# Layer 1's attention: the next unit's maxima taken before this unit's normalising, and a differential unit's first factor moved to its output rows

## The reference

```
def attend(q, k, v, scale):        # per block of 128 queries
    s = einsum('bqhd,bkhd->bhqk', qi, k) * scale
    p = softmax(s)
    return einsum('bhqk,bkhd->bqhd', p, v)

o_m = attend(q_m, k_m, v_m, MLA_SCALE)
a1  = attend(q1, k1, v_d, DIFF_SCALE)
a2  = attend(q2, k2, v_d, DIFF_SCALE)
o_d = rms_norm(a1 - lam * a2, g_sub) * (1 - lam_init)
y   = concat([o_m, o_d]) @ w_out
```

## Time and profile before

| | |
|---|---|
| median of 3 runs | 958.49 us (957.53 to 961.4) |
| profiled execution, span from first to last instruction | 954.8 us |
| PE busy | 851.6 us (89%) |
| DVE busy | 323.4 us (34%) |
| ACT busy | 170.0 us (18%) |
| the attention, from its first score matmul to the first of the output projection | 617.8 to 688.2 us |

### The profile page before, as it was taken

One profiled execution on the slowest core, in us unless ns is written; L12 is line 12 of the kernel. 1 busy time (PEld: TensorE's weight loads), 2 busy tenths in 40 slices (PEclk: granted clock), 3 DMA queues, 4 the chain that ended last, 5 costly groups with the idle time before them and its releaser, 6 DMA issues.

```text
span 954.8 us, 10284 instructions
## 1 busy us (share of the span) xinstructions
PE 851.6 (89%) x3887; PEld 376.0 (39%) x3887; DVE 323.4 (34%) x711; ACT 170.0 (18%) x419; POOL 170.5 (18%) x210
## 2 busy tenths in 40 slices
PE   4899999999999999868769999888899999779786
PEld 2444445447333333223257443354546333223222
DVE  1279997217111211111132441636405111011011
ACT  2301022115000000000042112445414000000000
POOL 2100391221220222220212211300110111011001
PEclk9899999999999999889969999999999999889898
DMA  9999454709999999999989024372657999999994
GB/s 362 408 414 388 152 211 186 300 35 324 328 407 405 372 400 375 420 400 417 374 361 387 1 100 165 135 307 107 281 230 265 381 406 409 418 418 425 413 418 180
DMA packets 33975, 298.00 MB, mean 312 GB/s; under 512 B 6560, under 2 KB 6866, under 8 KB 16252
## 3 DMA queue, kind: packets, MB, share of 16 engines
q1 hardware_dynamic: 26928, 283.26, 73.5%
q0 software_dynamic: 6912, 13.92, 4.1%
q10 hardware_dynamic: 76, 0.02, 0.0%
HBM read 293.66 MB, written 12.58 MB: 321 GB/s over the span
## 4 chain that ended last, share of the span: by engine, by line
PE 50%; DMA 21%; DVE 15%; issue 6%; ACT 3%; SPq 3%; PEld 2%; POOL 0%; another core or an unknown queue 0%; PEldq 0%; POOLq 0%; DVEq 0%
PE bank L1255 14%; DVE WORK L2156 9%; PE bank L473 9%; PE bank L1280 7%; DMA ring<-in_gu_pack 5%; PE bank L1405 5%; DMA B<-in_gu_pack 5%; DMA WORK<-in_gu_pack 4%; DMA ring<-in_win_pack 3%; PE bank L1133 3%; SPq L970 2%; PE bank L1352 2%; DVE small L1791 1%; PE bank L1029 1%; DMA h_rows<-B 1%
## 5 line engine op out<-in xcount | busy, mean ns | idle before, releaser
L1255 PE MATMUL bank<-ring,hT 128*64 128x512 f32 x688 | 210.5, 633 | 23.4 <-DMA ring<-in_gu_pack 16.6
L2070 DVE SCALAR_TENSOR_TENSOR hT<-hT,WORK,bank 128x256 f32<-128x256 f32 x34 | 16.3, 480 | 327.3 <-ACT hT L1556 327.3
L1255 PEld LDWEIGHTS bank<-ring,hT 128*64 128x64 f32 x688 | 62.1, 145 | 117.9 <-issue 117.7
L2156 DVE SCALAR_TENSOR_TENSOR WORK<-WORK,par 128x512 f32<-128x512 f32 x116 | 90.7, 861 | 0.0
L473 PE MATMUL bank<-ring,hT 128*128 128x512 f32 (+2 forms) x256 | 88.0, 499 | 0.7 <-ACT hT L1519 0.7
L1280 PE MATMUL bank<-ring,WORK 128*64 128x512 f32 x368 | 83.5, 595 | 1.6 <-ACT WORK L1561 1.6
L1255 PE MATMUL bank<-WORK,hT 128*64 128x512 f32 x128 | 59.8, 609 | 9.1 <-issue 7.6
L1561 ACT ACTIVATE WORK<-bank 128x256 f32<-128x256 f32 x34 | 13.1, 384 | 281.9 <-PE bank L1264 281.9
L1352 PE MATMUL bank<-hT,ring 128*128 128x512 f32 x128 | 58.4, 616 | 2.2 <-DMA ring<-in_win_pack 2.2
L473 PEld LDWEIGHTS bank<-ring,hT 128*128 128x128 f32 x256 | 46.0, 190 | 35.8 <-issue 34.0
L1029 PE MATMUL bank<-ring,cs 128*32 128x512 f32 x384 | 49.2, 638 | 9.5 <-DMA ring<-in_mod_pack 7.4
(11 more groups left out here) (297 smaller groups left out, 1039.1 us busy)
## 6 DMA issues: line engine op xcount, KB each, us to landing
ring<-in_gu_pack SPq DMA_DIRECT2D x38, 2048.0 KB, 22.3
ring<-in_mod_pack SPq DMA_DIRECT2D x24, 2048.0 KB, 12.8
ring<-in_down_pack SPq DMA_DIRECT2D x20, 2048.0 KB, 26.7
WORK<-in_gu_pack SPq DMA_DIRECT2D x6, 2048.0 KB, 32.7
ring<-in_wout_pack SPq DMA_DIRECT2D x4, 2048.0 KB, 15.7
ring<-in_gu_pack SPq DMA_DIRECT2D x8, 1024.0 KB, 28.0
ring<-in_win_pack SPq DMA_DIRECT2D x3, 2048.0 KB, 36.8
X<-in_gu_pack SPq DMA_DIRECT2D x3, 2048.0 KB, 30.3
```

The lines of the kernel that those rows point to most:

```text
L1255: mm = pe.matmul(dst[ST * x:ST * x + ST, :], HG[L][s][:, k, :], columns(units[x], 512 * k, 512), start=k == 0, stop=k == KC - 1)
L2070: dve.scalar_tensor_tensor(out=T1[L][s], in0=SG[L][s], scalar=cwt[:, at:at + 1], in1=src[:, 0:DE], op0=ALU.mult, op1=ALU.mult).then_inc(se ...
L2156: ins = dve.scalar_tensor_tensor(out=acc, in0=src, scalar=w, in1=acc, op0=ALU.mult, op1=ALU.add)
```

## The change

`maxima(0)` is taken before the loop, and iteration i on DVE becomes maxima(i+1), output_rows(i-2), normalize(i). `normalize` of a differential unit no longer scales the first map: it computes the second map's factor relative to the first (lam times the second reciprocal times the first sum) in one small instruction, and adds the second map to the unscaled first. The first map's factor `ri` goes to the output rows, which are multiplied by two factors in one instruction, and to the squares, as their input scale. The output rows of a differential unit therefore also wait for `probs_ready`.

```diff
@@ o_squares (ACT)
-                act.activation(OR[j], bank[5][:, 0:P], ACT.Square, accum_out=oss[:, j:j + 1]).then_inc(sem("o_squares"), 1)
+                u = 2 * (i % 4)
+                act.activation(OR[j], bank[5][:, 0:P], ACT.Square, scale=ri[:, u:u + 1], accum_out=oss[:, j:j + 1]).then_inc(sem("o_squares"), 1)
@@ normalize (DVE)
                 ins = dve.reciprocal(ri[:, u:u + 1 + d], es[:, o:o + 1 + d])
                 if d:
                     link(ins)
-                    tt(ri[:, u + 1:u + 2], ri[:, u + 1:u + 2], lam[:, 5:6], ALU.mult)
-                    link(ts(EX[:, i % 2, 0, :], EX[:, i % 2, 0, :], ri[:, u:u + 1], None, ALU.mult))
+                    link(dve.scalar_tensor_tensor(out=ri[:, u + 1:u + 2], in0=ri[:, u + 1:u + 2], scalar=lam[:, 5:6],
+                                                  in1=es[:, o:o + 1], op0=ALU.mult, op1=ALU.mult))
                     ins = dve.scalar_tensor_tensor(out=EX[:, i % 2, 0, :], in0=EX[:, i % 2, 1, :], scalar=ri[:, u + 1:u + 2],
                                                    in1=EX[:, i % 2, 0, :], op0=ALU.mult, op1=ALU.add)
@@ output_rows (DVE)
                 dve.wait_ge(sem("pv_mm"), i + 1)
+                dve.wait_ge(sem("probs_ready"), i + 1)
+                scale = ri[:, 2 * (i % 4):2 * (i % 4) + 1]
+                if i >= 2:
+                    dve.wait_ge(sem("o_turned"), i - 1)
                 if UNITS[i][0]:
                     dve.wait_ge(sem("o_rstd"), i - 7)
-                    scale = ors[:, i % 2:i % 2 + 1]
+                    ins = ts(OR[i % 2], bank[5][:, 0:P], scale, ors[:, i % 2:i % 2 + 1], ALU.mult, ALU.mult)
                 else:
-                    dve.wait_ge(sem("probs_ready"), i + 1)
-                    scale = ri[:, 2 * (i % 4):2 * (i % 4) + 1]
-                if i >= 2:
-                    dve.wait_ge(sem("o_turned"), i - 1)
-                ts(OR[i % 2], bank[5][:, 0:P], scale, None, ALU.mult).then_inc(sem("o_rows"), 1)
+                    ins = ts(OR[i % 2], bank[5][:, 0:P], scale, None, ALU.mult)
+                ins.then_inc(sem("o_rows"), 1)
+
+            maxima(0)
             for i in range(n_units + 2):
-                if i < n_units:
-                    maxima(i)
+                if i + 1 < n_units:
+                    maxima(i + 1)
                 if i >= 2:
                     output_rows(i - 2)
                 if i < n_units:
```

## The result

The changed kernel takes 983.8 us (median of 4 runs, 981.3 to 985.7) against 958.5 us (4 runs, 957.5 to 961.4). The ratio on record is 1.0255, with an interval of 1.0231 to 1.0280: some 25 us slower (24.4 by the ratio, 25.3 by the medians). The forecast was 974 us, with a range from 968.5 to 979.5. The sign and the new wait were right; the loss is 1.6 times the 15.8 us forecast.

What follows compares the result with a forecast made beforehand. The DVE-ACT chain (4.46 us a unit) was taken as the bound. Terms 15.7 - 2.4 - 0.6 + 2.6 + 0.4 + 0.1 = 15.8 us, added to 958.5, gave 974 us, range 968.5 to 979.5.

Steps and rivals of the forecast that it cites:

- The sign: Whole kernel: slower, given 91%, against 5% for same and 4% for faster.
- the new wait: Differential iterations 8 to 15: PE stands 1.96 us before values for output rows queued behind fresh maxima; +15.7 us.
- The latent units: Maxima of units 4 and 6 wait for fresh scores, output rows behind them: 1.31 us, twice; +2.6 us.
- Two factors in one scaling, the scaled squares: DVE output rows: 0.065 us in each of six places, +0.4 us; squares once at the end, +0.1 us.
- The scaling that went, at nothing: DVE's normalize in differential units: some 0.4 us saved each, counted as nothing because PE's stand covers it; 3.2 us at most.
- The sum of the waits: Attention up to the output projection's first matmul: 15.8 us later, 688.2 to 704.0 us.
- All of it reaches the end: Behind the attention: loads start later by the whole amount and cannot make it up, so all 15.8 us reach the span.
- The clock: PE in differential units: forecast keeps 2.4 GHz; rival has half the units at 1.2 GHz, 15 us more, 989 us, 6%.

Runs made afterwards that it cites:

- order_only: The kernel before with only DVE's order of the change, first map still scaled in normalize: 982.1 us, ratio 1.0258.
- rows_first: The changed kernel with output_rows(i-2) put before maxima(i+1) on DVE: 960.6 us, ratio 1.0013 to the kernel before.
- latent_order: The kernel before with DVE's order of the change in the latent units alone: 962.6 us, ratio 1.0033.
- factor_only: The changed kernel with DVE's old loop order, so only the factor is moved: 958.3 us against 958.2, ratio 1.0002.
- fillers: Matmuls nobody reads, added to the changed kernel on PE between scores and values in iterations 8 to 15: ratios 1.0204, 1.0189 and 1.0211 for seven, three and one.
- fill3: The changed kernel with three matmuls that nobody reads on PE in each of iterations 8 to 15: 975.5 us, ratio 1.0189 to the kernel before.
- fill7: The changed kernel with seven matmuls that nobody reads on PE in each of iterations 8 to 15: 977.3 us, ratio 1.0204 to the kernel before.
- fill1: The changed kernel with one matmul that nobody reads on PE in each of iterations 8 to 15: 978.3 us, ratio 1.0211 to the kernel before.

## Why the prediction missed

**The new wait: right.** The step from "DVE's maxima of unit i+1 need fresh scores" to "PE stands about 2 us before its values" came out as worked. The brackets of the rows say 1.98 us in the first three iterations and 2.11 in the others, 16.4 us in eight waits. Counted as in the prediction, from the scores' start less 1.06 us, it is 2.05 (651.29 - 648.18 - 1.06) and 2.17 (670.61 - 667.38 - 1.06), where 1.96 and some 2.03 were put. order_only and rows_first show the cause: with the order alone the whole loss is there, with output rows ahead of the maxima none of it.

**The latent units: right.** 1.33 and 1.36 us at two places where 1.31 was put. latent_order has them alone.

**Two factors in one scaling, the scaled squares: right.** The output rows of differential units take 410 ns against 350 for those of latent ones, 0.06 us where 0.065 was put; the square takes 368 ns against 277. The wait for them grew by more, 0.13 us, since these output rows also start later after their maxima (1.50 us, 668.55 to 670.05, against 1.43). That is within the upper bound that was given.

**The scaling that went, at nothing: right as put.** It was hidden by the new wait. Without the new wait it is worth 1.6 us in the attention (factor_only), less than the 3.2 us that I gave as the most it could be.

**The sum of the waits: right.** 15.8 us were put at the projection's first matmul. The profile with three fillers, at full clock in the attention, has 86.64 - 70.39 = 16.2 us: 13.7 in the differential units, where the terms make 13.2, and 2.6 in the latent ones.

**All of it reaches the end: right.** The part behind the attention was 1.5 us longer, not shorter, and the load that stood until 687.52 now stands until 713.19, when the last output rows are turned.

**The clock: wrong, and this is the step that failed.** It is the sentence "By these the short waits leave it at 2.4 GHz". With it the sum got no term for the clock. It rested on one stretch of 5 us, 621 to 626, in which PE was busy 63% of the time at a granted clock of 1.00. That stretch of the kernel before holds a single stand of 2 us and no row of them:

```profile
622.84 0.66 PE L550 MATMUL bank<-cst,GB 128*128 128x128 f32 x4 [1.97 <-DVE small L1800]
```

In the same paragraph I wrote that no stretch before shows such a share for 46 us, and still gave the case 6% and left its time out of the range. The changed kernel's clock first fell in the second differential iteration, and about half of the 42 us from 657 to 699 was run at the lower level. That cost 8.6 us of the attention's 24.8 in its profile: a little over half of the 15 us at which I had priced it. The Trainium skill (TensorE: Matmul & The Clock Gate, "A second HAM failure mode: psum-queue depth-cycling") states that short idle gaps between groups of matmuls can make the clock swing; this is the rule that I put aside for the row. The trace agrees with it: the first iterations take turns at 5.86, 7.47, 5.87 and 7.55 us, the next three are slow (9.31, of which 0.91 is a wait for the modulation, 7.75 and 7.44), the eighth is at full clock again, and no wait is longer than 2.1 us.

That it is the idle time, and not the order or contention, is shown by the fillers. They leave DVE's order and the time from scores to values as they are (3.10 us against 3.11) and take nearly all the slow iterations away.

By the times the share of the clock is less sharp. The changed kernel is 1.0255, the filled ones are 1.0189 to 1.0211, a difference of 4 to 6 us, with intervals of some 3 us to either side; the interval of fill3 is clear of the change's, that of fill7 touches it and that of fill1 overlaps. Taken together they are clear: the twelve runs of the filled kernels took 973.8 to 980.0 us, the eight of the changed kernel and order_only 981.0 to 987.4. Each filled profile has one fall left, of some 1.6 us (fill7 in the latent units, fill3 in the projection, fill1 at 688 us), so over attention and projection together the fillers save 7.0 us (122.9 to 115.9 or 116.0). And each filled kernel was profiled in the fastest of its four runs, so the 8.6 us may be somewhat too high for a typical run.

**Still open.** Where a fall lands differs between kernels whose attention hardly differs (projection 27.7 or 29.4 us), and probably between executions of one kernel; each was profiled once, so the place was not measured. The mean granted clock of each run hints at it: the four runs of fill3 took 973.8, 974.3, 976.7 and 980.0 us at 0.964, 0.964, 0.961 and 0.958, while the four of the changed kernel show no such order. What exactly makes the clock fall isn't settled either: the kernel with one filler, with stands of 1.56 and 1.69 us, had one fall.

## What to carry to other kernels

When work is taken a step ahead in an engine's queue and waits for a fresh input there, everything queued behind it becomes as late as that input. When a change makes TensorE stand in every iteration of a loop, price its clock as part of the loss, even where each stand is short: a stretch of the old trace with the same busy share was weak evidence here, since it held a single stand. Filling the stand with matmuls that nobody reads tests quickly how much of a loss is the clock.

## What the runs showed that was not expected

The clock fell with no stand of PE longer than 2.1 us, where PE was busy 24.2 of 35 us, part of it at the lower clock. With one added matmul in each iteration, by which the stand was 1.56 us instead of 1.98, it held for 35 us in which PE was busy for 25.2. And a kernel can get shorter by giving its busiest engine more to do: three useless matmuls in each of eight iterations took the ratio from 1.0255 to 1.0189.
